# When a quad's value rows are weighed and its row places given back, in the last stage of a two-block transformer kernel

## The reference, cut to what matters

```python
def chunk(args):
    xc, ec, gc = args
    u = u_tab[ec].astype(f32)
    act = jax.nn.gelu(jnp.einsum('ced,cd->ce', u, xc.astype(f32))) * gc
    return jnp.einsum('ce,ced->cd', act, v_tab[ec].astype(f32)).astype(x.dtype)
```

## Time and profile before

| | |
|---|---|
| median of 3 runs | 1906.92 us (1906.62 to 1916.26) |
| the profiled execution | 1915.19 us, span 1913.4 us |
| TensorE busy | 1751.5 us, 92% of the span |
| VectorE, ScalarE, GpSimd busy | 918.3, 454.1, 429.2 us |
| DMA | 620.32 MB, mean 324 GB/s |

### The profile page before, as it was taken

The page is one execution under the profiler, slowest core; times in us unless marked ns, Lnnn a source line. Parts: engine busy times, 40 slices in busy tenths (PEclk is TensorE's granted clock), DMA queues, the critical chain, the costliest instruction groups (busy, mean ns, idle before and its releaser), DMA issues. The chain is left out here.

```text
span 1913.4 us, 24225 instructions
## 1 busy us (share of the span) xinstructions
PE 1751.5 (92%) x9356; PEld 1120.9 (59%) x9356; DVE 918.3 (48%) x2234; ACT 454.1 (24%) x943; POOL 429.2 (22%) x312
## 2 busy tenths in 40 slices
PE   4989999988999999998899999998999888899898
PEld 4975444437887754442586557987777775333333
DVE  4467311124477841111698734988676643222222
ACT  5462211114345321110430424312111111000001
POOL 5820000005667500000200004323211221121110
PEclk9999899998999989999999999999999999999999
DMA  9986899995568769999632325499999999999996
GB/s 389 356 323 214 336 431 429 429 430 196 186 241 304 267 258 429 428 430 427 252 114 97 128 104 220 170 373 376 356 391 385 390 412 416 413 409 405 399 404 249
DMA packets 95093, 620.32 MB, mean 324 GB/s; under 512 B 11520, under 2 KB 12032, under 8 KB 60672
## 3 DMA queue, kind: packets, MB, share of 16 engines
q1 hardware_dynamic: 75824, 482.88, 63.3%
q0 software_dynamic: 18432, 134.23, 17.3%
q10 hardware_dynamic: 720, 1.61, 0.2%
HBM read 617.63 MB, written 1.05 MB: 323 GB/s over the span
## 5 line engine op out<-in xcount | busy, mean ns | idle before, releaser
L3114 PE MATMUL bank<-peer_tiles_a,peer_H 128*128 128x512 f32 x344 | 160.1, 606 | 18.4 <-DMA peer_tiles_a<-in_peer_v 18.4
L232 POOL TENSOR_TENSOR w_lo<-ring,w_hi 128x1024 fp32r<-128x1024 f32 x60 | 148.3, 2474 | 64.1 <-ACT w_hi L222 63.8
L3326 DVE CUSTOM_DVE_ANT_0 peer_junk<-peer_rows_b,bank 128x512 bf16<-128x512 f32 x128 | 83.2, 684 | 147.2 <-issue 118.3
L1096 PE MATMUL bank<-ring,moe_slots 128*64 128x512 f32 x576 | 131.5, 607 | 9.6 <-DMA ring<-in_stream 9.6
L3063 PEld LDWEIGHTS bank<-peer_xT,peer_tiles_a 128*128 128x128 f32 x1104 | 127.5, 192 | 17.8 <-issue 16.0
L3063 PE MATMUL bank<-peer_xT,peer_tiles_a 128*128 128x128 f32 x1104 | 135.1, 278 | 1.6 <-DMA peer_tiles_a<-in_peer_u 1.6
L3114 PEld LDWEIGHTS bank<-peer_tiles_a,peer_H 128*128 128x128 f32 x344 | 62.8, 191 | 107.1 <-issue 75.9
L3326 DVE CUSTOM_DVE_ANT_0 peer_junk<-peer_rows_a,bank 128x512 bf16<-128x512 f32 x96 | 61.1, 683 | 129.5 <-issue 118.3
L3221 ACT ACTIVATE peer_opened<-peer_pre 128x1 f32<-128x1 f32 x128 | 27.3, 284 | 401.3 <-DVE peer_pre L3326 401.3
L3178 POOL DMA_INDIRECT peer_rows_b<-in_peer_uv,peer_index x64 | 60.2, 940 | 249.0 <-PE bank L3094 234.1
L1277 DVE TENSOR_TENSOR bank<-bank,mod 128x512 f32<-128x512 f32 x32 | 22.4, 699 | 175.6 <-PE bank L1146 175.6
(11 more groups left out here) (515 smaller groups left out, 3632.7 us busy)
## 6 DMA issues: line engine op xcount, KB each, us to landing
ring<-in_stream SPq DMA_DIRECT2D x103, 2048.0 KB, 12.7
early<-in_stream SPq DMA_DIRECT2D x32, 2048.0 KB, 18.7
peer_tiles_a<-in_peer_v SPq DMA_DIRECT2D x86, 512.0 KB
peer_tiles_a<-in_peer_u SPq DMA_DIRECT2D x69, 512.0 KB
sb_mod_ring<-in_ada_t SPq DMA_DIRECT2D x64, 512.0 KB, 6.3
peer_tiles_b<-in_peer_v SPq DMA_DIRECT2D x42, 512.0 KB
peer_tiles_b<-in_peer_u SPq DMA_DIRECT2D x34, 512.0 KB
ret_mod_ring<-in_ada_t SPq DMA_DIRECT2D x32, 512.0 KB, 5.0
```

Of the source, the lines that this page charges most:

```text
L232: pool.tensor_tensor(self.shaped(self.w_lo, q, by_columns), self.quarter(n, q, by_columns), self.shaped(self.w_hi, q, by_columns).bitcast( ...
L1096: last = pe.matmul(K.bank[own(e), 4 + up, :], slots[:, f, own(2 * p + e)], w[:, e, k, :], start=(f == 0), stop=(f == KD - 1))
L3114: last = pe.matmul(K.bank[:, 2 + dh, :], H[:, m, :], first.slot(n)[:, dh * 512:(dh + 1) * 512], start=(m == 0), stop=(m == PK - 1))
L3326: dve.tensor_tensor_reduce(out=junk[:, g % 2, 0:512], in0=rows[i % ROWS_HELD][:, cols], in1=K.bank[:, 4 + g, :], scale=1.0, scalar=0.0, op ...
```

## The change

Only TensorE's order is changed. `weigh_half(p)` now weighs the quad of an odd p, which is the quad whose second half p is. Beside the picks it stands two tiles behind that half's spread (`n - 2`). In the key groups it stands behind the gate units that already wait for the same half's dots; the quads whose second half is the last of a group are weighed in the next group, behind its first tile. Among the value tiles it stands behind the fourth tile after the spread of the second half (`m - 3`). No instruction is added or taken away; SyncE's order is the same, and so is what the other engines issue.

```diff
             def weigh_half(p):
-                if p % 2 == 0 and p:
-                    values_of(p // 2 - 1)
+                if p % 2:
+                    values_of(p // 2)
...
-                if n - 1 in HALF_AT:
-                    weigh_half(HALF_AT[n - 1])
+                if n - 2 in HALF_AT:
+                    weigh_half(HALF_AT[n - 2])
             pe.wait_ge(dotted, 2 * BESIDE_PICKS)
             turn_picks(0, 6)
             pe.wait_ge(selT_made, 1)
...
                 spread_half(p)
                 keys(n)
-                weigh_half(p)
+                if e:
+                    weigh_half(p - 1)
                 keys(n + 1)
                 if m < UNITS:
                     gate_unit(m)
                     gate_unit(m + 1)
+                weigh_half(p)
                 keys(n + 2)
                 pe.wait_ge(h_gated, min(m + 2, UNITS))
                 spread_half(p + 1)
                 keys(n + 3)
-                weigh_half(p + 1)
                 keys(n + 4)
                 if m < UNITS:
                     gate_unit(m + 2)
                     gate_unit(m + 3)
+                weigh_half(p + 1)
                 keys(n + 5)
                 pe.wait_ge(h_gated, min(m + 4, UNITS))
                 spread_half(p + 2)
                 keys(n + 6)
-                weigh_half(p + 2)
                 keys(n + 7)
...
                 values(m)
-                for p in range(halves_before(m), halves_before(m + 1)):
-                    weigh_half(p)
-                if m == PK - 5:
-                    values_of(QUADS - 1)
+                if m == 0:
+                    weigh_half(VALUES_FROM // 2 - 1)
+                if m >= 3:
+                    for p in range(halves_before(m - 3), halves_before(m - 2)):
+                        weigh_half(p)
```

## The result

The changed kernel is slightly slower: 1917.24 us median (1912.77 to 1922.1, 20 runs) against 1912.51 us (1906.2 to 1917.99, 20 runs), ratio 1.0027 with a 95% interval of 1.0016 to 1.0039. That is 5 us, inside the bound of 0.5%, but on the other side of the 8.0 us that were forecast. The median lies above the 1912 us at which the range ends; carried over to the 1906.92 us from which the forecast started, the ratio gives 1912.1 us, the range's upper end.

The account below looks back on a forecast made before the run. DMA near full was taken as the bound, with hollows at the releases. Key groups -8.0, picks 0, value tiles 0 gave -8.0 us: 1907.2 us profiled, 1898.9 us on the median, range 1888 less 3 to 1912 us.

Parts of the forecast that it names:

- What bounds the stage: Last stage: DMA near full at 416 GB/s, 50.4 us per cycle of two key groups; TensorE, busy 48.6 us, not the floor.
- The key groups, -8.0 us: Key groups: earlier weighings fill the gather hollows (6.2 us together) and some of the rest; -8.0 us, bounds 0 and 12.3.
- Beside the picks, "I take 0": Picks' stretch: late first gate pair against earlier gathers of quad 5; 0, bounds 4 us of loss and 5.6 of gain.
- 1 to 2 us each: Beside the picks: the three weighings before quad 3's wait 1 to 2 us each, making its weights little over a microsecond later.
- paid by a wait that was there: Pair at 1383.76 us: the 4 us delay is absorbed by TensorE's 2.98 us wait; done at 1386.5 instead of 1387.2 us.
- The signs of being wrong: Cycles of 54 us with the hollow; first gate pair after 1352 us, cycle end later than 1387; key-tile waits (L3063).
- The value tiles, 0: Value tiles: every quad is weighed 1.7 tiles and a spread earlier; 0, bounds 1 us of loss and 5 of gain.
- The pattern only shifts: Value tiles: releases stay 9 or 10 tiles apart, so hollows only shift; 1.1 us lost at the end, about as much gained.
- Slower by the wait beside the picks: Rival at quad 3's weighing: 4 to 6 us of loss stay, key groups may gain nothing; +5 to +7, 1913 us, chance 0.06.
- The hollows only move: Rival: gaps of 4, 5, 7 tiles keep the old hollow in the long one; 0 to -2, 1906 us, chance 0.26.
- Starved tiles: Rival: tiles longer at 127 GB/s, TensorE waits at key tiles; about +2, or +6 with picks, 1909 to 1913 us, chance 0.06.
- The rule that a DMA engine goes round the queues packet by packet: Against the change: a never-empty gather queue leaves tiles their smaller share all the time; no size beyond the starved-tiles rival's.

Follow-up runs that it names:

- e2: Only the key groups in the new order, picks and value tiles as before, against the kernel before: ratio 0.9945, 10.5 us faster.
- e1: Only the weighings of quads 0 to 3 beside the picks moved early, all else old, against the kernel before: ratio 1.0063, 12 us slower.
- e4: Key groups and value tiles in the new order, picks in the old, against the kernel before: ratio 0.9974, 5 us faster.
- e5: On top of e2, quads 0 to 2 weighed early beside the picks, quad 3 not: ratio 0.998 to the kernel before, 6.7 us slower than e2.
- e6: On top of e2, quad 3 alone weighed early beside the picks: ratio 0.9984 to the kernel before, 7.4 us slower than e2.
- e3: Only the value tiles in the new order, all else old, against the kernel before: ratio 1.0017, 3 us slower.
- e8: On top of e4, quad 19's weighing, second among the value tiles, put two tiles later: ratio 0.9968 to the kernel before, not told apart from e4.

## Why the prediction was right or wrong

**What bounds the stage** was right. Where the new order works, the DMAs run at 414 to 416 GB/s and three of the four cycles stand near the 50.4 us that were worked out for them.

**The key groups, -8.0 us**, was right in mechanism and a little small: -10.5 us alone. The filled hollows show, so does the backlog of gathers that carries the full rate over the long gap, and the waits of 3 to 4 us are down to 2.1 in e2 and 1.8 in the changed kernel. Part of the gain isn't seen in the cycles: the fourth is longer than before, and the bytes moved ahead in it come back among the value tiles. The earlier trace rows also ended 2.75 us short of the first value tile, so the bound of 12.3 us was 2.75 too small. What the prediction did not see is that the two moved quads of a cycle are one measure: it priced each hollow by itself, as if each early release were worth its own.

**Beside the picks, "I take 0"**, is the step that failed: 12 us of loss by e1 and 10 from e4 to the changed kernel; the bounds were 4 of loss and 5.6 of gain. Without it the change would have been faster, as e4 is. Two parts of it were wrong.
- *Quads 0 to 2 were counted as stalls of "1 to 2 us each"* that left only "a little over a microsecond" at quad 3. Two of the three stalls had that size (1.58 and 1.56 us), the first had 4.34. What was missing is what such a stall does to VectorE. The early weighing closes a loop: spread of the second half, VectorE's dots behind a head's picks, ScalarE's weights, the weighing, one key tile, the next spread, and VectorE's next dots, which now wait for that spread. The old order let the next spread go ahead of the weighing, and VectorE never stood waiting for it (e2). e5 shows it: 7.5 us of waits on TensorE, 10.3 on VectorE, and 6.7 us of time from these three quads alone.
- *The debt was to be "paid by a wait that was there"*, the 2.98 us at 1383.76 us. That wait is for rows which quad 4's release brings, and quad 4's release is late when the first gate pair is late. e1 shows it: wait and debt both stand, 12 us in all. Of the 10 us by which quad 5's gathers were to start earlier, 2 to 3 were left behind the first spread, and they bought nothing that the time shows: the gathers of quad 6 started 8 us later than before and 12 later than in e2, GpSimd stood 24.28 us waiting for that release, and the hollow of 1340 us only moved to 1360 (156 GB/s for 10 us). For quad 3 by itself the arithmetic of the transposes was good (6.3 us late, 6.7 found in e6), but the first gate pair was 6.2 late and not 4.

That the transposes stand at 1346.30 us, near the 1345 that was given as a sign of being right, is luck: the whole stretch began 6.4 us earlier in that execution. The signs of being wrong came too, a first gate pair after 1352 us (1353.34), a cycle end later than 1387 us (1388.70) and waits for key tiles.

**The value tiles, 0** with a bound of 1 us of loss, was too kind: 3 us alone (e3), 5.5 on top of the key groups (e4 against e2), with wide intervals. The microsecond lost while TensorE works alone at the end (1.1 foreseen) agrees with the 1.3 estimated from the rows; no run measures it by itself. "The pattern only shifts" is true of the gaps from quad 20 on, but the first two gaps become 7 and 10 tiles, 14.9 and 29.6 us in the changed kernel, with the hollow of 266 GB/s behind them. e8 moved the long gap and did not remove it, so whether the gaps are the loss is not shown. Where the other 2 to 4 us lie is open.

**The rivals.** "Slower by the wait beside the picks" named the place, quad 3, and had the point from which it decides right (less paid back at 1383 us than is lost at 1347), at 0.06. Its +5 to +7 us hold the measured +5 by luck: it had 4 to 6 us of loss beside the picks and no gain in the key groups, where 12 and -10.5 were found. "The hollows only move" was true beside the picks and false in the key groups. Starved tiles did show in groups 8 and 9, where TensorE now waits for key tiles (2.4 us the longest); since the DMAs run at their full rate there, and e2 has such waits too (up to 1.7 us) and gains 10.5, this reads as a symptom and not as a loss, though no run tested it.

The rule that a DMA engine goes round the queues packet by packet (the Trainium skill, DMA: Bandwidth & Descriptors, Queues, rings and completion order) was weighed as a case against the change. The trace agrees with it where both queues had work (478 and 407 packets); the fourth cycle at 60.6 us and 415 GB/s shows the tiles late, at the full rate.

## What to carry to other kernels

Giving a buffer back earlier gained here where its refill was late for someone, and only when the next release in the ring was earlier as well; with the first alone the wait went to the consumer of the next, and with the second alone it stayed. Before an instruction is moved ahead on an in-order engine, follow the whole loop through the other engines once around: if the moved one waits for work that itself waits for what now stands behind it, each turn can add a stall. And an idle wait further on pays for a delay only if what it waits for isn't delayed too.

## What was not expected of the hardware

Two queues that both have work share the packets evenly, but not the bytes, and not only in the window of the earlier trace rows. In e4 from 1616 to 1628 us the gathers, in rows of 8 KB, had 452 packets with 3.31 MB and the tiles, in rows of 4 KB, 458 with 1.66 MB: two thirds of the bytes for the gathers, and 3.8 us for a tile, an estimate from that rate. It holds only while gathers are waiting. From 1632 to 1636 us, with none left, the tiles had 97.9% of the engines' time, so that over the 28 us shown above they come to 230 GB/s. A rate read from a short window tells what a tile costs beside gathers, and not how long it stays that way.
